# Peeling the first and last group out of an expert loop, and splitting the last weight transfer

## What is computed

```
x  = x + g1 * (mixers(h) @ w_out)
h2 = rms(x, norm2_g) * (1 + sc2) + sh2
# top-1 of 4 expert groups, then top-2 of its 8 experts; gate per token and expert
y  = sum over the two experts e of a token: gate[e] * ((silu(h2 @ w1[e]) * (h2 @ w3[e])) @ w2[e])
out = x + g2 * y
```

## Time and profile before

| what | value |
|---|---|
| median of 3 runs | 1635.98 us (1635.53 to 1637.23) |
| span of the profiled execution (no other time of it is given) | 1640.1 us |
| TensorE matmul busy | 1370.1 us (84%) |
| VectorE busy | 650.7 us (40%) |
| chain that ended last | DMA 50%, TensorE 44%, VectorE 5% |
| of the chain, transfers of expert weights | ring 34%, Zpad 9%, tail 3% |
| transfers of expert weights | 192 of 2048 KB |

### The profile page before, as it was taken

One profiled execution on the slowest core, in us unless ns is written; L12 is line 12 of the kernel. 1 busy time (PEld: TensorE's weight loads), 2 busy tenths in 40 slices (PEclk: granted clock), 3 DMA queues, 4 the chain that ended last, 5 costly groups with the idle time before them and its releaser, 6 DMA issues.

```text
span 1640.1 us, 18412 instructions
## 1 busy us (share of the span) xinstructions
PE 1370.1 (84%) x7629; PEld 803.5 (49%) x7629; DVE 650.7 (40%) x968; ACT 194.9 (12%) x482; POOL 30.5 (2%) x35
## 2 busy tenths in 40 slices
PE   5999999999999999998777677677678677767767
PEld 4668888678888758863323123123123123213223
DVE  4557783799873568432221120120121121212213
ACT  2002212211122011130100100100001001001001
POOL 0000100000000000010000000000000000000000
PEclk9999999999999999999888888798787788888888
DMA  9997787667866776989999999999999999999996
GB/s 397 427 427 291 295 335 300 256 269 283 336 250 250 281 275 278 380 356 381 430 428 428 428 428 428 428 428 428 428 428 428 428 429 428 428 428 429 428 428 291
DMA packets 44539, 611.94 MB, mean 373 GB/s; under 512 B 4896, under 2 KB 5168, under 8 KB 6736
## 3 DMA queue, kind: packets, MB, share of 16 engines
q1 hardware_dynamic: 42848, 604.00, 88.6%
q0 software_dynamic: 1072, 6.44, 0.9%
q10 hardware_dynamic: 576, 0.89, 0.2%
HBM read 609.21 MB, written 2.10 MB: 373 GB/s over the span
## 4 chain that ended last, share of the span: by engine, by line
DMA 50%; PE 44%; DVE 5%; issue 1%; SPq 0%; ACT 0%; DVEq 0%
DMA ring<-in_exp_w 34%; PE W L714 14%; DMA Zpad<-in_exp_w 9%; PE W L691 7%; DMA ring<-in_stream 5%; PE M L1150 5%; DMA tail<-in_exp_w 3%; DVE tail L1513 2%; PE A L1168 2%; PE W L1031 2%; PE W L665 2%; PE W L1058 2%; PE W L699 2%; PE W L1102 1%; PE M L675 1%; PE W L1115 1%
## 5 line engine op out<-in xcount | busy, mean ns | idle before, releaser
L1150 PE MATMUL M<-ring,g1b 128*32 128x512 f32 x1280 | 183.9, 706 | 76.8 <-DMA ring<-in_exp_w 76.6
L1513 DVE SCALAR_TENSOR_TENSOR tail<-ring,small,tail 128x512 f32<-128x512 f32 x300 | 225.6, 752 | 10.5
L1446 DVE TENSOR_TENSOR consts<-A,tail 32x512 f32<-32x512 f32 x128 | 87.9, 686 | 162.0 <-PE A L1168 159.0
L1150 PEld LDWEIGHTS M<-ring,g1b 128*32 128x32 f32 x1280 | 38.9, 120 | 186.9 <-DMA ring<-in_exp_w 113.3
L2051 DVE SCALAR_TENSOR_TENSOR tail<-tail,M 128x128 f32<-128x128 f32 x32 | 9.2, 288 | 298.8 <-ACT tail L1423 298.8
L1168 PE MATMUL A<-Zpad,tail 128*32 128x512 f32 x512 | 88.1, 820 | 31.5 <-DMA Zpad<-in_exp_w 24.2
L691 PE MATMUL W<-buf_h,ring 128*128 128x256 f32 x512 | 111.9, 379 | 0.0
L1122 PEld LDWEIGHTS M<-consts,tail 128*128 128x128 f32 x512 | 65.7, 201 | 93.0 <-ACT tail L1425 60.3
L714 PE MATMUL W<-ring,buf_x 128*128 128x256 f32 x480 | 108.7, 384 | 2.3 <-DVE ring L1446 2.3
L691 PEld LDWEIGHTS W<-buf_h,ring 128*128 128x128 f32 x512 | 96.7, 190 | 12.9
L714 PEld LDWEIGHTS W<-ring,buf_x 128*128 128x128 f32 x480 | 91.8, 192 | 15.5 <-DVE ring L1446 2.5
(11 more groups left out here) (333 smaller groups left out, 1371.9 us busy)
## 6 DMA issues: line engine op xcount, KB each, us to landing
ring<-in_exp_w SPq DMA_DIRECT2D x96, 2048.0 KB, 36.7
ring<-in_stream SPq DMA_DIRECT2D x88, 2048.0 KB, 12.2
Zpad<-in_exp_w SPq DMA_DIRECT2D x56, 2048.0 KB, 38.0
PPY<-in_exp_w SPq DMA_DIRECT2D x24, 2048.0 KB, 30.7
tail<-in_exp_w SPq DMA_DIRECT2D x16, 2048.0 KB, 45.2
Zpad<-in_early SPq DMA_DIRECT2D x8, 1536.0 KB, 10.6
buf_x<-in_x SPq DMA_DIRECT2D x2, 1024.0 KB, 6.9
buf_h<-in_x POOLq DMA_DIRECT2D x1, 2048.0 KB, 12.2
```

The source lines that it names most:

```text
L1150: ins = pe.matmul(M[32 * j:32 * j + 32, 512 * w13:512 * w13 + 512], XT[:, kk, 32 * q:32 * q + 32], w[:, 512 * k:512 * k + 512], start=(kk ...
L1446: return dve.tensor_tensor(o, x, y, op)
L1513: ins = dve.scalar_tensor_tensor(acc, w, cs[:, kk:kk + 1], acc, ALU.mult, ALU.add)
```

## The change

It does five things.

1. The loop over groups is no longer two nested loops but the first group, a loop over the groups between, and the last group, written out three times from one function `expert_group(it, place)` on TensorE, ScalarE and VectorE; SyncE's loop is cut in the same way. The count in `cnt_i` becomes the number of inner groups (here 6), with one more VectorE instruction; shifting a group's positions by 32 for the next round is now done per group, on 4 columns.
2. The first group has no scatter. GpSimd's clearing of `GT` and `ysb` goes away.
3. The last group has no gather and no dressing. In its place, ahead of q = 3, TensorE scatters the 96 rows of its first three experts: token half 1 into `W` (4 products, then a VectorE add into `x1`), and for token half 0 four products of `x1` with the identity and four of the scatter, summed in `W`.
4. The very last half, j23, comes in two transfers of 1 MB with a semaphore each.
5. The last expert's result is multiplied by g2 in one instruction on 128 partitions, and scattered by 8 products that use 32 rows of the array each, with a turned gate matrix repeated four times (`tail_GT`, made behind q = 0 of the last group: two VectorE copies, two more turns on TensorE and one ScalarE copy). ScalarE copies the sum for token half 0 from `W` to `x1` (4 instructions), VectorE adds token half 1 (4 instructions).

SyncE and TensorE, core of the diff:

```diff
+                if in_pieces:
+                    sp.dma_start(place[:, 0:2048], w[4 * g + q, hf][:, 0:2048]).then_inc(full, 16)
+                    sp.dma_start(place[:, 2048:4096], w[4 * g + q, hf][:, 2048:4096]).then_inc(sem["tail_piece"], 16)
+                else:
+                    sp.dma_start(place, w[4 * g + q, hf]).then_inc(full, 16)
...
-            pool.memset(GT, 0.0).then_inc(sem["gt_ready"], 1)
...
-                pool.memset(ysb[32 * q:32 * q + 32, :], 0.0).then_inc(sem["y_copied"], 4)
...
+            def scatter_early(dst, tt, b, alone):
+                return pe.matmul(dst, GT[0:96, tt * P:tt * P + P], ysb[0:96, 512 * b:512 * b + 512],
+                                 start=alone, stop=alone)
...
+                    if q == 3 and place != 'final':
+                        pe.wait_ge(sem["g_ready"], it + 2)
+                        if place != 'first':
+                            pe.wait_ge(sem["y_added"], 2 * it)
+                        gather()
+                    elif q == 3:
+                        pe.wait_ge(sem["gt_ready"], it + 2)
+                        pe.wait_ge(sem["y_copied"], 16 * it + 12)
+                        for b in range(4):
+                            ins = scatter_early(W[:, 512 * b:512 * b + 512], 1, b, True)
+                        ins.then_inc(sem["scattered"], 1)
+                        pe.wait_ge(sem["y_added"], 2 * it + 1)
+                        for b in range(4):
+                            d = slice(512 * b, 512 * b + 512)
+                            pe.matmul(W[:, d], ident, x1[:, 0, d], start=True, stop=False)
+                            scatter_early(W[:, d], 0, b, False)
...
+                            if place == 'final' and (q, hf, c2) == (3, 1, 1):
+                                pe.wait_ge(sem["tail_piece"], 16)
+                            ins = expert_down(w, 2 * hf + c2, c2)
...
-                            scatter(it)
+                        if place != 'first':
+                            scatter_former(it)
...
+                        if place == 'final':
+                            pe.wait_ge(sem["g_ready"], it + 2)
+                            pe.wait_ge(sem["y_added"], 2 * it)
                             for tt in range(TT):
+                                ins = pe.transpose(W[:, tt * P:tt * P + P], tail_rows[:, tt * P:tt * P + P], ident)
                             ins.then_inc(sem["g_turned"], 1)
...
+            pe.wait_ge(sem["y_copied"], 16 * final + 13)
+            for tt in range(TT):
+                for m in range(4):
+                    dst = W[:, 512 * m:512 * m + 512] if tt == 0 else M[:, 512 * m:512 * m + 512] if m < 3 else A[:]
+                    pe.matmul(dst, tail_GT[32 * m:32 * m + 32, tt * P:tt * P + P], part[32 * m:32 * m + 32, :],
+                              start=(tt == 1), stop=True).then_inc(sem["scattered"], 1)
```

ScalarE and VectorE at the end:

```diff
+            for m in range(4):
+                d = slice(512 * m, 512 * m + 512)
+                act.wait_ge(sem["scattered"], 2 * final + (2 + m))
+                act.activation(x1[:, 0, d], W[:, d], ACT.Copy).then_inc(sem["tail_kept"], 1)
...
+                    if q == 3 and place == 'final':
+                        dve.wait_ge(sem["scattered"], 2 * it + 1)
+                        tt_op(x1[:, 1, :], W[:], x1[:, 1, :], ALU.add).then_inc(sem["y_added"], 1)
...
+                    if q == 3 and place == 'final':
+                        tt_op(part, A[:], g2c, ALU.mult).then_inc(sem["y_copied"], 1)
...
-            for b in range(4):
-                d = slice(512 * b, 512 * b + 512)
-                dve.wait_ge(sem["scattered"], 16 * rounds + (2 * b + 1))
-                tt_op(x1[:, 0, d], W[:, d], x1[:, 0, d], ALU.add).then_inc(sem["out_ready"], 1)
-                dve.wait_ge(sem["scattered"], 16 * rounds + (2 * b + 2))
-                tt_op(x1[:, 1, d], M[:, d] if b < 3 else A[:], x1[:, 1, d], ALU.add).then_inc(sem["out_ready"], 1)
+            for m in range(4):
+                d = slice(512 * m, 512 * m + 512)
+                dve.wait_ge(sem["scattered"], 2 * final + (6 + m))
+                tt_op(x1[:, 1, d], M[:, d] if m < 3 else A[:], x1[:, 1, d], ALU.add).then_inc(sem["out_ready"], 1)
```

More of the change, by code:

```diff
@@ L2069, in _ @@
-                        dve.wait_ge(half_used, PER_GROUP * it + (PE_BASE + 6 * q + 6))
+                            dve.tensor_scalar(used_pos, used_pos, -32.0, None, ALU.add)
+                            tt_op(Gg, Gm, column(gate3, c), ALU.mult).then_inc(sem["g_ready"], 1)
+                    elif q == 3 and place != 'final':
+                        for b in (1, 3):
+                            dve.wait_ge(sem["gathered"], 4 * it + (b + 5))
+                            dress_tokens(b)
+                    dve.wait_ge(half_used, PER_GROUP * it + (PE_BASE + 6 * q + 6))
```

259 lines of the change are left out of this document (136 added, 123 removed).

## The result

| what | before | changed |
|---|---|---|
| median, 22 runs each side by side | 1637.06 us (1632.23 to 1643.13) | 1641.63 us (1638.59 to 1644.3) |
| ratio, 95% interval | | 1.0027 (1.0016 to 1.0037): 4.4 us slower |
| profiled execution: span | 1640.1 us | 1636.5 us |
| its own time | about 1641.9 us (worked out) | 1638.63 us |

The time is more than the span by 1.7 to 1.9 us in the executions of before, and by 1.9 to 2.1 in those of the changed kernel; 0.2 us of the difference thus lies outside the spans. The two spans alone say "3.6 us faster"; the medians say 4.6 us slower.

The account below looks back on a forecast made before the run. The prediction took the stream of expert weights, at 428 to 430 GB/s, to bound the kernel. 1640.1 - 4.4 + 2.9 - 1.1 = 1637.5 us for the profiled execution, carried over to a median of 1633.4 us; range 1630.2 to 1637.0.

Parts of the forecast that it names:

- The first group: -4.4 us.: Without the first group's scatter, j17 is issued earlier and the transfer hole at 760 to 766 us closes, saving 4.4 us.
- the large hole: Stretch at 760 to 766 us where the profiled transfers move only 111 GB/s; closing it was valued at 4.4 us.
- The loop's cutting itself adds nothing to a stage in which all engines wait for weights.: In the expert stream, cutting the loop over groups in three was taken to cost 0.
- The last group, ahead of q = 3: +2.9: Waits and 12 products ahead of the last q = 3 cost 0.2 us, plus 2.7 for the lowered clock.
- Behind the last product: -1.1: From last product to first store, row-group products take 3.6 us instead of 4.7; the end moves by -1.1 us.
- The rivals on row groups: At the kernel's end the row-group products don't run side by side: +1.2 instead of -1.1, 1635.7 us; chance 0.10.
- the PSUM copies: Rival: copies out of PSUM, not the stores, set the end: -3.2 instead of -1.1, 1631.3 us; chance 0.03.
- I carry the difference over: 1633.4: Whole kernel: the median lies 4.1 us below the profiled span, so the sum of 1637.5 becomes 1633.4 us.

Follow-up runs that it names:

- first_cut: Kernel before with only the first group taken out of the loop, without its scatter of zeros and GpSimd's clearing; ratios to before 0.9999 and, repeated, 0.9994.
- b_third: The kernel before, unchanged, run again for a third profile; ratio to before 0.9990.
- cut_only: Kernel before with all its work, the loop cut in three, plus the changed kernel's group count and position shift; 1640.41 us and, repeated, 1639.54 us.
- filled: Changed kernel with products of no use added in TensorE's two breaks ahead of the last group's q = 3; ratio to before 1.0017.
- b_again: The kernel before, unchanged, run again for a second profile; 1637.84 us, ratio 1.0000.
- late: Changed kernel without the 12 early products, tail_GT and row groups, with the end of the kernel before; 1636.83 us, ratio 1.0001 (repeated: 1.0011).

## Why the prediction was wrong

Point by point, by its own steps:

- **"The first group: -4.4 us."** Mechanism right, size not the kernel's. In first_cut the stream gains just this against a profile with the large hole, but b_third shows that the hole is large or small by the clock, and there 877.8 was reached with the scatter in place. Against the mean of three profiles of before (880.1) the changed kernel's stream gains 2.1; without its late landing of some 1.5 it would be 3.6.
- **"The loop's cutting itself adds nothing to a stage in which all engines wait for weights."** This is the step that failed outright, and no rival had it. cut_only costs 3.3 us by the ratios. By the landings 1.3 to 1.6 us of it lie in the stream; where the rest lies is open. Engines that wait for weights hide their own work, not what their instruction fetches do to the transfers.
- **"The last group, ahead of q = 3: +2.9."** Mechanism right and undersized. Without clock effects I had 10.49 + 8.7 = 19.2 us from j17 to q = 3, with them 21.9. The three profiles took 21.4, 22.8 and 23.4; filled took 18.1. Against filled the clock takes 3.3 to 5.3, not 2.7. From q = 3's first product to the end of its last one the first profile took 14.04 us, where I had 14.05.
- **"Behind the last product: -1.1."** Right: 3.6 to the first store against 4.7, two row-group sets in about 1 us each, no wait for j23, and 7.4 us from the first store to the end in both kernels. With the term ahead of q = 3, the last part took 47.6 us against 44.6 in the means of three, +3.0 where the sum has +1.8. The rivals on row groups and on the PSUM copies fell.
- **"I carry the difference over: 1633.4."** This step turned a sum of 1637.5, for a span that came out as 1636.5, into a forecast that missed by 8 us. 1640.1 was no typical execution of before. It is 5.6 us longer than b_third, 3.5 of them in the stream with the full hole and 1.7 ahead of j9. But the hole alone doesn't make an execution slow: b_again has it too, with a span of 1637.0. A saving read from that execution was taken off a median that was already 4 us below it, and 1635.98, the median of three runs, lay 1.1 us below that of 22.

In the means of three profiles each: j9 issued +1.1, stream -2.1, last part +3.0, together +2.0, as the mean spans (1639.2 against 1637.2). The medians differ by 4.6. The rest is mostly that the three profiles of before lie 2 us above its median (those of the changed kernel 0.4 below theirs), and the 0.2 us outside the spans; which of the parts is shorter in its median execution can't be seen.

No variant beats both kernels beyond the uncertainty. first_cut (0.9999 and 0.9994) is the nearest; late, with the whole change but its end, equals before.

## What to carry to other kernels

Before forecasting a change of 0.3%, look at how the profiled execution stands to the median: a hole that the clock made is not a saving of the kernel. Writing a loop's body out more than once is not free in a stage bound by transfers (shown here for three and more copies, and for a loop body of two and four groups): look at the instruction queue's packets there, and at the spacing of the landings, since the mean share of the transfer engines stays at 1.01. Work that is moved off the end must fit where it goes, and a break ahead of it is paid twice, as a wait and as clock.

## What the runs showed of the hardware

- A loop body of one group isn't fetched again (31 packets in all); one with two or four groups is, in each pass (68 and 64), and the kernel takes 7 us of 1637 more.
- Late landings come in steps of 0.6 to 1.6 us, with a packet of 16 KB of the instruction queue in the stretch or just ahead of it, while the 16 engines' mean share reads 1.01.
- After the same break of 2.38 us the same four products took 3.70 us in b_third and 5.20 in the first profile of before. In filled the clock fell in q = 3's w2 products (2.94 us instead of 1.92) behind a wait of only 0.38 us. The kernel's executions spread over 11 us (1631.85 to 1643.32), those of the changed kernel over 6.
- Products with K = 32 in four row groups, 512 columns in f32, run side by side: a set of four in about 1 us, where one product of 128 rows takes 0.86.
